# Latent attention and its output projection as three rounded products, and another order of VectorE and ScalarE at the end of an expert item

## What is computed

```
q   = rmsnorm(cq) @ w_uq             # 8 heads, 128 plain + 64 rotary columns each
k   = [ckv @ w_uk | kr]              # 128 per head + 64 rotary columns shared by the heads
o   = softmax(q k^T / sqrt(192)) v   # context reads 128 keys, latent tokens 640
mix = o @ w_out                      # (640, 1024) @ (1024, 1024)
y  += gate_e * (silu(x @ w_g) * (x @ w_u)) @ w_down   # for two experts of each token
```

## Time and profile before

| | us |
|---|---|
| median of 3 runs | 2620.74 (2617.67 to 2621.68) |
| the profiled execution | 2624.85 |
| its span in the profile | 2623.0 |
| TensorE busy in it | 2340.0 |

### The profile page before, as it was taken

The page is one execution under the profiler, slowest core; times in us unless marked ns, Lnnn a source line. Parts: engine busy times, 40 slices in busy tenths (PEclk is TensorE's granted clock), DMA queues, the critical chain, the costliest instruction groups (busy, mean ns, idle before and its releaser), DMA issues.

```text
span 2623.0 us, 34735 instructions
## 1 busy us (share of the span) xinstructions
PE 2340.0 (89%) x14062; PEld 1997.1 (76%) x14063; DVE 1025.0 (39%) x1463; ACT 883.1 (34%) x1251; POOL 472.2 (18%) x266
## 2 busy tenths in 40 slices
PE   6999887848899999989889999969999888899894
PEld 4896665538778999989866566669898788798783
DVE  2421264545713212142101343143346666645434
ACT  3320244211105111131222232133346666645444
POOL 0100002462002000020000000033214454423211
PEclk8989978669999999999999999969999999899996
DMA  6121104931521212111211000026547888757554
GB/s 281 50 89 48 56 1 171 343 120 49 180 78 48 81 65 81 61 56 67 87 44 51 17 1 0 0 92 243 188 171 288 318 323 307 300 206 271 213 182 160
DMA packets 70057, 353.34 MB, mean 135 GB/s; under 512 B 12112, under 2 KB 17872, under 8 KB 37296
## 3 DMA queue, kind: packets, MB, share of 16 engines
q1 hardware_dynamic: 65200, 337.28, 34.8%
q0 software_dynamic: 4736, 14.26, 1.5%
HBM read 318.06 MB, written 33.46 MB: 134 GB/s over the span
## 4 chain that ended last, share of the span: by engine, by line
PE 62%; issue 15%; POOL 9%; DVE 6%; ACT 4%; DMA 3%; SPq 0%; POOLq 0%; DVEq 0%; ACTq 0%
PE ps L562 59%; POOL wring_x L1897 5%; PE ps L699 1%; PE ps L965 1%; ACT arena L1017 1%; POOL tmp L1121 1%; DVE tmp L1406 1%; POOL tmp L1119 1%; POOL arena_x L1608 1%; DVE att L987 1%; DVE tmp L1346 1%; DMA xT<-in_x 1%; DMA wring<-in_w_mod 1%; POOL rows L2080 0%; ACT hT L690 0%
## 5 line engine op out<-in xcount | busy, mean ns | idle before, releaser
L1897 POOL TENSOR_TENSOR wring_x<-wring,arena_x 128x2048 fp32r<-128x2048 f32 (+1 forms) x60 | 276.5, 4616 | 480.4 <-ACT arena_x L1891 480.3
L562 PE MATMUL ps<-arena_x,hT_x 128*128 128x256 f32 x2464 | 325.6, 289 | 12.0 <-issue 7.3
L562 PEld LDWEIGHTS ps<-arena_x,hT_x 128*128 128x128 f32 x2464 | 307.9, 194 | 15.7 <-issue 13.3
L1891 ACT ACTIVATE arena_x<-wring 128x2048 fp32r<-128x2048 f32 x153 | 283.4, 1854 | 91.0 <-DMA wring<-in_w_mgu 90.8
L562 PE MATMUL ps<-hT,wring 128*128 128x320 f32 x1088 | 302.5, 441 | 12.3 <-ACT hT L690 10.6
L562 PE MATMUL ps<-arena_x 128*128 128x320 f32 (+2 forms) x1336 | 283.4, 365 | 29.1 <-DVE arena_x L2066 13.3
L562 PEld LDWEIGHTS ps<-hT,wring 128*128 128x128 f32 x1088 | 210.6, 194 | 104.3 <-issue 20.2
L562 PEld LDWEIGHTS ps<-arena_x 128*128 128x128 f32 x1336 | 232.5, 200 | 59.8 <-issue 25.7
L1897 DVE TENSOR_TENSOR wring_x<-wring,arena_x 128x2048 fp32r<-128x2048 f32 (+1 forms) x90 | 223.0, 2478 | 73.4 <-ACT arena_x L1891 73.4
L562 PE MATMUL ps<-arena 128*128 128x128 f32 (+3 forms) x680 | 176.8, 421 | 7.1 <-ACT arena L1017 4.8
L562 PE MATMUL ps<-tmp_x,arena_x 128*128 128x320 f32 x1024 | 165.7, 314 | 6.0 <-ACT hT L690 6.0
(11 more groups left out here) (294 smaller groups left out, 2989.6 us busy)
## 6 DMA issues: line engine op xcount, KB each, us to landing
wring<-in_w_mgu SPq DMA_DIRECT2D x105, 1024.0 KB, 6.4
wring<-in_w_mod SPq DMA_DIRECT2D x48, 1024.0 KB, 8.7
wring<-in_w_mdn SPq DMA_DIRECT2D x30, 1024.0 KB, 4.9
wring<-in_w_gu SPq DMA_DIRECT2D x22, 1024.0 KB, 4.8
wring<-in_w_mdn SPq DMA_DIRECT2D x20, 768.0 KB, 4.3
wring<-in_w_ev SPq DMA_DIRECT2D x14, 1024.0 KB, 4.9
rows<-hT SPq DMA_DIRECT2D x1, 12288.0 KB, 34.5
wring<-in_w_dn SPq DMA_DIRECT2D x16, 704.0 KB, 4.1
```

The lines of the kernel that those rows point to most:

```text
L562: return nc.tensor.matmul(out, lhsT, rhs, start=first, stop=last)
L1891: nc.scalar.activation(whi[b % 6][:, 0:wsize(b)], wslot[s][:, 0:wsize(b)], ACT.Copy).then_inc(whi_ready, 1)
L1897: eng.tensor_tensor(wslot_x[s][:, 0:size], wslot[s][:, 0:size], whi[b % 6][:, 0:size].bitcast(F32), ALU.subtract).then_inc(ready, 1)
```

## The change

Scores and output projection become rounded products. `qn`, `kn`, the rotary parts, the attention's output and `w_out` are split in hi and lo. The rests of the key heads 0 to 5 lie in `wring` slots that the output weights use later, so three of their four loads now wait for the scores that read them last. Half of the output weights is split during the last items of the attention, half behind it. At the end of an expert item two operations of ScalarE and several of VectorE change places.

```diff
         krT, ckv, cq = arena[:, 19968:19968 + TK], chunks(20736, 2, TK), chunks(22272, 3, T)
         krraw = arena[:, 24192:24192 + T]
+        qn_hi, qn_lo, qr_hi, kn_hi = exact(0, HC, T), fh[1], exact(5120, 4, T), exact(7680, HC, TK)
+        qr_lo = [fh[0][:, 4 + c, :] for c in range(4)]
+        kr_hi, kr_lo = arena_x[:, 22272:22272 + TK], arena_x[:, 23040:23040 + TK]
+        qrope = chunks(15104, 2, T)
+        o_hi, o_lo = fh[1], exact(0, HC, T)
+        oohi = [arena_x[:, base:base + WB] for base in (7680, 9984, 13824, 15872)]
         pC = tmp[:, 0:2 * T].rearrange("p (b t) -> p b t", b=2)
         aC = tmp[:, 2 * T:4 * T].rearrange("p (b t) -> p b t", b=2)
-        qraw = tmp[:, 4 * T:6 * T].rearrange("p (b t) -> p b t", b=2)
+        qraw = chunks(13824, 2, T)
 
         g_, beta, gcum, glast, eg, ed, el = (dsm[:, i, :, :, :] for i in range(7))
...
+            if stage == "oo" and 2 * turn + j < 3:
+                full(sync, "att1", plan_c.index(("scores", (4 * turn + 2 * j + 1) * NT + NT - 1, 0)))
...
+            if c < 6:
+                s, _ = wuse("oo", c // 2 % 2, c // 4)
+                return wring_x[:, s, c % 2 * TK:(c % 2 + 1) * TK]
+            base = (23808, 19968)[c - 6]
+            return arena_x[:, base:base + TK]
 
...
+        def attention(heads, streams, stage, order, scores, values, probs, turned, item_base, first_width, take_out,
+                      act_more=lambda eng, i: None, dve_more=lambda eng, i: None):
...
-                            terms = scores(h, t, st_, 0, P)
+                            terms = scores(h, t, st_, 0, first_width)
                             for n, (q, k) in enumerate(terms):
-                                last = mm(ps[:, s, 0:P], q, k, n == 0, n == len(terms) - 1)
+                                last = mm(ps[:, s, 0:first_width], q, k, n == 0, n == len(terms) - 1)
...
-                        nc.vector.tensor_copy(hT[:, stat + h, t * P:(t + 1) * P], ps[:, s, 0:P]
-                                              ).then_inc(ps_free[s], 1)
+                        take_out(st, h, t, ps[:, s, 0:P]).then_inc(ps_free[s], 1)
+                    dve_more(eng, i)
...
+                    act_more(eng, i)
...
         def mla_scores(h, t, st_, a, b):
-            r = slice((h % 2) * ROPE, (h % 2 + 1) * ROPE)
-            return [(qn[:, h, t * P:(t + 1) * P], kn[:, h, a:b]), (qr[r, h // 2, t * P:(t + 1) * P], krT[r, a:b])]
+            r, m, q = slice((h % 2) * ROPE, (h % 2 + 1) * ROPE), h // 2, slice(t * P, (t + 1) * P)
+            return [(qn_hi[:, h, q], kn_hi[:, h, a:b]), (qn_hi[:, h, q], kn_lo(h)[:, a:b]), (qn_lo[:, h, q], kn_hi[:, h, a:b]),
+                    (qr_hi[r, m, q], kr_hi[r, a:b]), (qr_hi[r, m, q], kr_lo[r, a:b]), (qr_lo[m][r, q], kr_hi[r, a:b])]
+        def mla_out_parts(st, h, t, src):
+            hi = o_hi[:, h, t * P:(t + 1) * P]
+            st.then(nc.vector.tensor_copy(hi, src))
+            return nc.vector.tensor_tensor(o_lo[:, h, t * P:(t + 1) * P], src, hi.bitcast(F32), ALU.subtract)
...
+        def act_oohi(act, n, part):
+            s, use = wuse("oo", n % 2, n // 2)
+            act.wait_ge(w_full[s], 16 * (use + 1))
+            a = slice(part * 1024, part * 1024 + 1024)
+            nc.scalar.activation(oohi[n][:, a], wring[:, s, a], ACT.Copy).then_inc(oohi_ready, 1)
+        def dve_oolo(dve, n, part):
+            dve.wait_ge(oohi_ready, 2 * n + part + 1)
+            s, _ = wuse("oo", n % 2, n // 2)
+            a = slice(part * 1024, part * 1024 + 1024)
+            nc.vector.tensor_tensor(wring_x[:, s, a], wring[:, s, a], oohi[n][:, a].bitcast(F32), ALU.subtract
+                                    ).then_inc(oolo_ready, 1)
+        def act_early_oo(act, i):
+            if OO_ITEM <= i < OO_ITEM + 4:
+                act_oohi(act, (i - OO_ITEM) // 2, (i - OO_ITEM) % 2)
+        def dve_early_oo(dve, i):
+            if OO_ITEM < i <= OO_ITEM + 4:
+                dve_oolo(dve, (i - OO_ITEM - 1) // 2, (i - OO_ITEM - 1) % 2)
+        OO_ITEM = 6 * NT + NT - 1
+        def act_late_oo(act):
+            full(act, "att1", len(plan_c) - 1)
+            for n in (2, 3):
+                for part in range(2):
+                    act_oohi(act, n, part)
+        def dve_late_oo(dve):
+            for n in (2, 3):
+                for part in range(2):
+                    dve_oolo(dve, n, part)
+        def pe_oo():
+            for n in range(4):
+                s_w, _ = wuse("oo", n % 2, n // 2)
+                for c in range(2):
+                    s = take("oo", 2 * (n % 2) + c, n // 2)
+                    for prod, (w, h) in enumerate(((oohi[n], o_hi), (oohi[n], o_lo), (wring_x[:, s_w, :], o_hi))):
+                        for k in range(KD):
+                            if c == 0 and prod != 1 and k % 4 == 0:
+                                nc.tensor.wait_ge(oolo_ready if prod else oohi_ready, 2 * n + k // 4 + 1)
+                            for half in range(2):
+                                last = mm(pair(s)[:, half, :], w[:, k * 256 + c * P:k * 256 + (c + 1) * P],
+                                          h[:, k, half * HT:(half + 1) * HT], prod + k == 0, prod == 2 and k == KD - 1)
+                    filled(last, "oo", 2 * (n % 2) + c, n // 2)
...
         att1 = attention(HC, 1, "att1", plan_c, mla_scores, lambda h, b: vC[:, b, h * P:(h + 1) * P],
-                         lambda i, s: pC[:, i % 2, :], lambda i: aC[:, i % 2, :], H * NT, 0)
+                         lambda i, s: pC[:, i % 2, :], lambda i: aC[:, i % 2, :], H * NT, 256, mla_out_parts,
+                         act_early_oo, dve_early_oo)
...
-                nc.scalar.activation(qn[:, c, :].rearrange("p (b n) -> p b n", b=2), pair(s), ACT.Copy, scale=scale
-                                     ).then_inc(ps_free[s], 1)
+                nc.scalar.activation(qn_hi[:, c, :].rearrange("p (b n) -> p b n", b=2), pair(s), ACT.Copy, scale=scale
+                                     ).then_inc(qkhi_ready, 1)
...
-                nc.scalar.activation(kn[:, c, :].rearrange("p (b n) -> p b n", b=2), pair(s, TK // 2), ACT.Copy
-                                     ).then_inc(ps_free[s], 1)
+                nc.scalar.activation(kn_hi[:, c, :].rearrange("p (b n) -> p b n", b=2), pair(s, TK // 2), ACT.Copy
+                                     ).then_inc(qkhi_ready, 1)
...
+            for c in range(HC):
+                dve.wait_ge(qkhi_ready, c + 1)
+                s, _ = R.use("uqn", c)
+                nc.vector.scalar_tensor_tensor(
+                    qn_lo[:, c, :].rearrange("p (b n) -> p b n", b=2), pair(s), 192 ** -0.5,
+                    qn_hi[:, c, :].bitcast(F32).rearrange("p (b n) -> p b n", b=2), ALU.mult, ALU.subtract
+                    ).then_inc(ps_free[s], 1)
             for c in range(4):
...
-                dve_rope(st, qraw[:, c % 2, :], qr[:, c, :], s)
+                dve_rope(st, qraw[:, c % 2, :], qrope[:, c % 2, :], s)
+                done(dve, "uqr", uq_order.index(("R", c)))
+                st.then(nc.vector.tensor_copy(qr_hi[:, c, :], qrope[:, c % 2, :]))
+                nc.vector.tensor_tensor(qr_lo[c], qrope[:, c % 2, :], qr_hi[:, c, :].bitcast(F32), ALU.subtract
+                                        ).then_inc(rope_lo_ready, 1)
+            dve.wait_ge(mla_caches_in, 32)
+            st.then(nc.vector.tensor_copy(kr_hi, krT))
+            nc.vector.tensor_tensor(kr_lo, krT, kr_hi.bitcast(F32), ALU.subtract).then_inc(rope_lo_ready, 1)
+            for c in range(HC):
+                dve.wait_ge(qkhi_ready, HC + c + 1)
+                if c == 7:
+                    dve.wait_ge(rope_lo_ready, 5)
+                    dve.wait_ge(mla_out, 32)
+                s, _ = R.use("kn", c)
+                nc.vector.tensor_tensor(
+                    kn_lo(c).rearrange("p (b n) -> p b n", b=2), pair(s, TK // 2),
+                    kn_hi[:, c, :].bitcast(F32).rearrange("p (b n) -> p b n", b=2), ALU.subtract
+                    ).then_inc(ps_free[s], 1)
...
+                    act_ahi(act, EC - 2, i)
                     act_whi(act, EC + 3, i)
-                    act_ahi(act, EC - 2, i)
+                    act_ahi(act, EC - 1, i)
                     act_whi(act, EC + 4, i)
-                    act_ahi(act, EC - 1, i)
                     act_xhi(act, 0, i)
                     act_xhi(act, 1, i)
                     act_whi(act, EC + 5, i)
...
-                        if j + 2 not in POOLS:
+                        if j + 2 not in POOLS and j < EC - 1:
                             write_wlo(dve, j + 2, i, wlo_ready)
...
+                    write_wlo(dve, EC + 1, i, wlo_ready)
                     dve_alo(dve, EC - 3, i)
-                    write_wlo(dve, EC + 3, i, wlo_ready)
                     dve_alo(dve, EC - 2, i)
                     dve_alo(dve, EC - 1, i)
-                    write_wlo(dve, EC + 4, i, wlo_ready)
+                    write_wlo(dve, EC + 3, i, wlo_ready)
+                    dve_y(dve, 0, i)
```

(26 more changed lines are left out.)

## The result

The median went from 2619.2 us (four runs) to 2586.1 us (four runs, 2584.2 to 2589.5): ratio 0.9877, 95% interval 0.9852 to 0.9902. The kernel is faster, as forecast, but by 1.2% where 2.6% was forecast, and the time lies 6 us above the top of the range (2580). The profiled execution took 2584.36 us, its span is 2581.9 (before: 2624.85 and 2623.0).

A forecast was written before the change was run, and what follows sets the result against it. TensorE's work and its gaps were taken to bound the kernel. 12.6 + 11 + 13 + 23 + 14 - 5 = 68.6 off 2624.85, less 4.1, gave 2552 us; range 2542 to 2566, with rivals 1 to 3 2534 to 2580.

The forecast's parts named there:

- Experts, 45 us: Expert stage: two waits removed (13 and 23 us) and clock regained (14), less 5 for later loads: 45 us saved.
- The wait ahead of `xt2`: End of each expert item: `dve_y(0)` ahead of the row rests saves 2.3 us in ten items, 23 us.
- that ahead of `dn0`: Six small expert items: splitting block 12 after the slot is freed and the product saves 2.2 us each, 13 us.
- the 5 for what is late next: Between small expert items: weight loads and GpSimd's rests become late, taking back 1.3 to 1.7 us in four items, 5.
- The 14 for the clock: Expert stage: with both gaps down to half a microsecond, slow clock behind them returns 14 us, bounds 0 and 23.
- Rival 1: Expert stage paced by loads and GpSimd: clock gives 0, pacing takes 14 of 36, 22 remain; 2575 us, chance 0.22.
- Projection, 12.6 us: Output projection: fp32r products take 56.1 us instead of 69.14, 13.0 less, hand-over costs 0.4: net 12.6 us saved.
- Scores, 11 us: Attention scores: 2.43 us instead of 2.84 in 32 items, four shape changes kept, 13.1 less 2 for splits: 11 saved.
- rival 4: Attention and output projection: granted clock falls in the rounded products, kernel slower, about 2692 us; chance 0.01.
- Rival 3: Scores' shape change free with fp32r, or the whole experts' clock returns: 9 to 22 us more gain, say 2535; chance 0.09.
- Rival 2: VectorE binds the attention: a take-out 0.4 us dearer loses the scores' 11 us; 2563 us, chance 0.08.
- Projections ahead, 0: Projections ahead of the attention: VectorE's added rests fit TensorE's rhythm, cost 0; 1 to 3 us if one head late.

The follow-up runs named there:

- e4: Kernel before the change with 33 idle TensorE instructions added, moving its expert loop to the changed kernel's place (0.234 of a 16 KB piece): 2645.8 us, ratio 1.0082.
- e5: Changed kernel with 204 TensorE instructions behind a skipped branch ahead of the expert loop, which then starts 0.03 into a 16 KB piece: 2552.3 us, ratio 0.9757.
- e1: Kernel before the change with only the new order of VectorE and ScalarE at the end of an expert item, TensorE's program untouched: 2585.1 us, ratio 0.9857.
- e3: Changed kernel with 223 executed TensorE wait instructions added, moving its expert loop back to the old place (0.105 of a piece): 2581.3 us, ratio 0.9838.
- e6: Changed kernel with 223 TensorE instructions behind a skipped branch, putting its expert loop at the old place (0.105 of a piece): 2557.5 us, ratio 0.9783.
- e12: e8 with each tile's twelve score products grouped by operand shape, two changes of shape in place of four: 2537.8 us, ratio 0.9700.
- e8: e5 with TensorE's wait for the value copies moved from the attention's start to ahead of the first product with values: 2546.8 us, ratio 0.9744.

## Why the prediction was wrong

- **The step that failed** is one the sum does not have. It costs the instructions that the rewritten products issue where they run, and "Cost 0" stands where they lie beside other work; nowhere does it ask what TensorE's longer program does to the code behind it. The new place of the expert loop cost 22.4 us of gaps (11.9 to 34.3; 2.0 of it ahead of the first item, where no fetch lies) and up to 10.4 of slow clock behind them. e4 charges 21 us for it on the kernel before, and e5 gets 32 us back in the expert stage. The miss of the forecast is 34 us. In the profiles the expert stage is 25.2 us longer in after than in e1, where the loop has its old place, and the slow start of the attention, below, lost 8.5: 33.7 together.
- **Experts, 45 us.** Right in its terms where the code has its old place: 47 in e1's profile, and in the changed kernel 16.8 + 5.6 in place of it. The wait ahead of `xt2` went from 27.1 to 5.4 (forecast 23 saved), that ahead of `dn0` to nothing (13), and the 5 for what is late next was 5.8 in GpSimd's rests. The 14 for the clock came (busy time 709.93 before, 694.77 in e1: 15.2), but in after 5.6 of it went again to the gaps' slow clock. The working named one reading by which this 14 would be near 0; that did not come. Rival 1 had a time of 2575 for another cause. After lies 11 us above it, and what GpSimd's rests took was 5.8 of the 14 that it named.
- **Projection, 12.6 us.** Measured 12.6.
- **Scores, 11 us.** Mechanism right: the change of shape stays (2.51 us against 2.43), and heads run at 18.0 us against 18.2. Of that only 3.2 showed, since the start of the attention ran at half clock for 17 us; without it the profile would have given 11.7 (3.2 + 8.5). The prediction's rival 4 thought of a falling clock and put it down to the kind of product. In the runs it follows the wait ahead of it, with the old product too, and passes after 10 to 17 us.
- **Rival 3** came in part, where the code lies well: the experts' clock is 0.99 in e5. **Rival 2**, VectorE binding the attention, did not come: in six heads TensorE is busy 108.00 of 108.00 us.
- **Projections ahead, 0.** The 3.4 us found there are within what this point of the program varies by from profile to profile.
- Of the signs named at the end, the projection, the heads and the vanished wait ahead of `dn0` came as said, and the wait ahead of `xt2` fell to 5.4 and not under 5. Only three of six small items took 55 to 57 us; the three others took 60 to 61, and in two of these a gap of over 5 us ahead of the next item is counted. The clock of 0.97 or 0.98 would not have caught the miss: it was 0.97. The sign that does is the "issue" row of TensorE's waits.

## What to carry to other kernels

If an engine's loop is larger than what it can hold of its program, the place of the loop counts: a change that adds instructions anywhere ahead of it may move 20 to 30 us into or out of the loop's turns. Before such a change is judged, compare the "issue" gaps at the loop's top and the packets of the instruction queue, and try one or two shifts behind a skipped branch. And group products by operand shape: each change of shape was 0.18 to 0.19 us of TensorE's time here.

## What the runs showed of the hardware

- TensorE's program comes in 16 KB packets; a loop of 8.8 of them ran with 25 to 40 fetches over ten items, by its place. Items of the kind just run need none (four small ones in a row). Where a packet's start lay in the gap ahead of `gu0`, TensorE idled for 5.1 to 5.9 us, and once (e3) for 8.6; where it lay a little ahead of the gap, for 0.6 to 4.8. `gu0` came 4.0 to 5.5 us behind the packet's start each time. Behind a long gap the matmuls run at 1.2 GHz at first (3.77 us for 2.08).
- The same place did not always give the same gaps: e3 and e6 both lie at 0.105, and e3 had an 8.59 us gap ahead of its second item where e6 had 1.44. What else counts (what ran just ahead, or where the program lies in memory) is open.
- 446 waits on a semaphore long full, in 223 instructions, took 20.4 us on TensorE, 0.09 an instruction.
- The granted clock fell to half while TensorE was busy without a gap, 2.4 to 2.6 us behind a wait of 1.3 us in ten profiles of twelve, and stayed there for 10 or 17 us. Behind a wait of 2.0 to 2.2 us near the end of the attention it fell in e6 and e12 and stayed in after and e8. What decides is open.
